# Bidirectional scan of a Mamba-2 layer: where the decay exponents are built, and by which engine

## The reference

```python
a_cs = jnp.cumsum(dt * a_head, axis=2)
seg = a_cs[:, :, :, None] - a_cs[:, :, None, :]
decay = jnp.exp(jnp.where(lower, seg, -jnp.inf))
y_diag = einsum(cb[..., None] * decay, x * dt)
chunk_states = einsum(bmat, decay_end, x * dt)
y_off = einsum(cmat, s_in, jnp.exp(a_cs))
y = y_f + flip(y_b) + xs * p['d'][:, None]
y = y * silu(z)
```

## Time and profile before

| | us |
|---|---|
| median of 3 runs | 1374.57 (1373.78 to 1378.78) |
| the profiled execution, its own time | 1375.81 |
| its span in the profile | 1374.0 |
| PE busy in the span | 1204.2 (88%) |
| DVE busy | 805.6 (59%) |
| ACT busy | 649.9 (47%) |
| POOL busy | 523.4 (38%) |

### The profile page before, as it was taken

How to read it: one execution, slowest core, us unless ns; L and a number is a source line. 1 busy time by engine, 2 the same in 40 slices (tenths; PEclk the granted TensorE clock), 3 DMA queues, 4 the chain that set the end, 5 groups by cost and what they waited for, 6 DMA issues and landing times.

```text
span 1374.0 us, 17386 instructions
## 1 busy us (share of the span) xinstructions
PE 1204.2 (88%) x6304; PEld 951.4 (69%) x6304; DVE 805.6 (59%) x1047; ACT 649.9 (47%) x1131; POOL 523.4 (38%) x233
## 2 busy tenths in 40 slices
PE   4799878877899999999789999677778889999998
PEld 1675453447567877778689999555557866777778
DVE  2546894473247887874467710687864024688782
ACT  2524113363425666765465533656644132466661
POOL 0513220022005545455135554577644500545650
PEclk9799798988999999999899999877789999899999
DMA  8644149940226888884113333544410302688961
GB/s 352 234 153 153 62 175 357 422 167 1 107 96 229 298 285 316 275 279 179 70 64 123 123 123 123 130 127 130 145 54 1 153 16 104 213 284 304 321 241 46
DMA packets 80031, 241.68 MB, mean 176 GB/s; under 512 B 6624, under 2 KB 38880, under 8 KB 67168
## 3 DMA queue, kind: packets, MB, share of 16 engines
q1 hardware_dynamic: 76336, 235.43, 48.3%
q10 hardware_dynamic: 3632, 5.42, 1.2%
HBM read 236.36 MB, written 4.46 MB: 175 GB/s over the span
## 4 chain that ended last, share of the span: by engine, by line
PE 56%; issue 12%; DVE 11%; POOL 7%; ACT 7%; DMA 6%; SPq 1%; ACTq 0%; DVEq 0%; POOLq 0%
PE bank L1887 10%; PE bank L1889 9%; PE bank L1888 9%; POOL wlo L667 4%; PE bank L2396 4%; PE bank L1911 3%; PE bank L2145 3%; DMA raw<-experts 3%; PE bank L2269 2%; POOL wlo L650 2%; DVE wlo L1630 2%; PE bank L2154 2%; PE bank L1955 2%; DVE ct L1767 1%; ACT whi L769 1%
## 5 line engine op out<-in xcount | busy, mean ns | idle before, releaser
L650 POOL TENSOR_TENSOR wlo<-raw,whi 128x2048 fp32r<-128x2048 f32 x39 | 178.7, 4586 | 360.9 <-ACT whi L769 360.9
L1630 DVE TENSOR_TENSOR wlo<-raw,whi 128x1024 fp32r<-128x1024 f32 x144 | 251.7, 1772 | 37.0 <-ACT whi L1004 35.5
L1004 ACT CAST whi<-raw 128x1024 fp32r<-128x1024 f32 x216 | 225.4, 1052 | 97.1 <-PE bank L1889 48.5
L667 POOL TENSOR_TENSOR wlo<-raw,whi 128x1024 fp32r<-128x1024 f32 x72 | 203.2, 2823 | 170.3 <-ACT whi L1004 170.3
L1887 PE MATMUL bank<-hhi,whi 128*128 128x384 f32 (+1 forms) x504 | 175.4, 348 | 16.6 <-DVE hlo L1297 7.2
L1888 PE MATMUL bank<-hlo,whi 128*128 128x384 f32 (+1 forms) x504 | 172.8, 343 | 0.0
L1889 PE MATMUL bank<-hhi,wlo 128*128 128x384 f32 (+1 forms) x504 | 172.7, 343 | 0.0
L1887 PE MATMUL bank<-whi,blk_hi 128*128 128x512 f32 x288 | 116.7, 405 | 2.6 <-issue 1.4
L1888 PE MATMUL bank<-wlo,blk_hi 128*128 128x512 f32 x288 | 114.3, 397 | 0.0
L1889 PE MATMUL bank<-whi,blk_lo 128*128 128x512 f32 x288 | 114.0, 396 | 0.0
L1887 PEld LDWEIGHTS bank<-hhi,whi 128*128 128x128 f32 (+1 forms) x504 | 95.6, 190 | 26.7 <-issue 10.8
(11 more groups left out here) (340 smaller groups left out, 2348.4 us busy)
## 6 DMA issues: line engine op xcount, KB each, us to landing
raw<-experts SPq DMA_DIRECT2D x216, 512.0 KB, 4.8
raw<-stream SPq DMA_DIRECT2D x61, 1024.0 KB, 4.9
modw<-core_mods SPq DMA_DIRECT2D x32, 1024.0 KB, 8.4
rowb<-acs_rows SPq DMA_DIRECT2D x48, 256.0 KB, 4.9
shared<-shared SPq DMA_DIRECT2D x6, 1024.0 KB, 7.9
s<-s0T SPq DMA_DIRECT2D x8, 256.0 KB, 4.3
new_s<-pf SPq DMA_DIRECT2D x16, 128.0 KB, 3.5
x<-xT ACTq DMA_DIRECT2D x1, 1536.0 KB, 13.7
```

Source lines behind the costliest of these rows:

```text
L650: pool.tensor_tensor(wlo[:, q % SPL, :], raw[:, pos % RAW, :], whi[:, q % SPL, :].bitcast(F32), ALU.subtract).then_inc(lo_done, 1)
L667: pool.tensor_tensor(unit(wlo, j), unit(raw, j), unit(whi, j).bitcast(F32), ALU.subtract).then_inc(ls.e_lo[j % SLOTS], 1)
L1004: act.copy(unit(whi, j), unit(raw, j)).then_inc(ls.e_hi, 1)
L1630: dve.tensor_tensor(unit(wlo, j), unit(raw, j), unit(whi, j).bitcast(F32), ALU.subtract).then_inc(ls.e_lo[j % SLOTS], 1)
```

## The change

- The exponents are no longer clamped on DVE. The cumulative sums and log(dt) minus them are written, each as a rounded part and a rest, to DRAM (`lines_out`, `nb_out`; one new PE job `nbT`), and SP brings per group 10 rows for each tile into `lines_f` (`fetch_lines`, six small transfers; one constant table of 74x1280 once). ACT rounds them into `lines` (`lines_cast`).
- PE `differences(n)` makes, for each direction, the exponent of four heads in PSUM by a product over ten rows, and adds a table `never` (0 or -1e30) by a product with the identity, so that the triangle is in the exponent. For t above 0 a product over two rows broadcasts the cumulative sum into another bank. Banks 4 to 7 hold these; the scan's jobs have four banks instead of six.
- ACT makes one exponential of 128x512 per direction out of PSUM into `seg`, and one into `ce` for t above 0. `seg` has two buffers instead of three.
- The C-B product is copied once, without triangle (`cb`).
- The skip term leaves PE: DVE `skipped` adds D times x to the result (two scalar_tensor_tensor of 128x128), and `gated` multiplies by z one tile later.
- Of `weighted_x`, the two products of tile 0 move from POOL to ACT (`scaled_x`, eight of 128x64); POOL does its other two at t = 2. POOL's quarter steps of weights go two at a time at t = 0.
- `turned(0)` and `differences(0)` stand before the last pair of z (`zw7`).

```diff
-    add(turned(0) + states(0))
+    add(numbered("xs", 8) + ["nbT"] + numbered("xs", XCH)[8:])
+    add(numbered("z", XCH)[:14] + turned(0) + numbered("z", XCH)[14:] + states(0))
...
+        b = turn % (CORE_BANKS if n in core else SCAN_BANKS if n in scan else JOB_BANKS)
...
-SOW_AT = {9: "sow3", 16: "sow4", 23: "sow5"}
+SOW_AT = {6: "sow3", 12: "sow4", 18: "sow5"}
...
+    def fetch_lines(hg):
+        for t in range(TILES):
+            ts = slice(t * P, (t + 1) * P)
+            at = 32 * t
+            sp.dma_start(lines_f[at:at + 2, 0:1024].rearrange("p (h l) -> p h l", h=8),
+                         rows_dram[8 * hg:8 * hg + 8, :, ts].rearrange("h a l -> a h l")).then_inc(lines_in, 16)
+            sp.dma_start(lines_f[at + 2:at + LINE_K, 1024:].rearrange("p (d l) -> p d l", d=2),
+                         cols_dram[8 * hg:8 * hg + 8, :, ts].rearrange("(d h) a l -> (h a) d l", d=2)).then_inc(
+                lines_in, 16)
...
-    sp.wait_ge(acs_out, 16)
-    taken(sp, JOB["z15"])
-    fetch_rows(0)
-    fetch_rows(1)
+    sp.wait_ge(lines_stored, 32)
+    sp.dma_start(lines_f[0:LINE_ROWS, :], inp["lines"]).then_inc(lines_k_in, 16)
+    sp.wait_ge(lines_k_in, 16)
+    fetch_lines(0)
+    sp.wait_ge(conv_out, 24)
     fetch_state(0)
+    sp.wait_ge(lines_set, 1)
+    fetch_lines(1)
     for n in range(TILES * 2 * SSD_G):
         hg, t = divmod(n, TILES)
-        if n >= 2:
-            finished(sp, JOB[f"y{(n - 2) // TILES}_{(n - 2) % TILES}"])
-        if n + 2 < TILES * 2 * SSD_G:
-            fetch_rows(n + 2)
+        finished(sp, JOB[f"y{hg}_{t}"])
+        if t == 1 and hg + 2 < 2 * SSD_G:
+            sp.wait_ge(lines_set, hg + 2)
+            fetch_lines(hg + 2)
...
+        if t == 2 and hg + 1 < 2 * SSD_G:
+            weighted_x(hg + 1)
+        if t == 0 and hg < 6:
+            for _ in range(2):
+                low_step(SPLIT_NO["sow0"] + nlow_steps // LOW_STEPS, nlow_steps % LOW_STEPS)
+                nlow_steps += 1
...
+    def scaled_x(hg):
+        if hg:
+            finished(act, JOB[f"st{hg - 1}_1"])
+        for dr in range(2):
+            for i in range(4):
+                h = dr * 32 + 4 * hg + i
+                w = slice(i * 64, (i + 1) * 64)
+                ins = act.activation(xw[:, dr, w], xtok[:, hg % 2, 0, w], ACT.Identity, bias=0.0,
+                                     scale=wdt[:, 0, h:h + 1])
+            ins.then_inc(xw_scaled, 1)
+    def lines_cast(hg):
+        act.wait_ge(lines_in, 16 * 2 * TILES * (hg + 1))
+        act.copy(lines[0:LINE_ROWS, hg % 2, :], lines_f[0:LINE_ROWS, :]).then_inc(lines_set, 1)
+    act.wait_ge(lines_stored, 32)
     turned_out(0)
+    split_to("sow0")
+    lines_cast(0)
+    z_out(7)
+    act.wait_ge(wdt_ready, 1)
+    taken(act, JOB["xt0_1"])
+    scaled_x(0)
+    split_to("sow2")
+    for n in range(TILES * 2 * SSD_G):
+        hg, t = divmod(n, TILES)
+        if n >= SEGS:
+            finished(act, JOB[f"y{(n - SEGS) // TILES}_{(n - SEGS) % TILES}"])
+        for dr in range(2):
+            act.wait_ge(seg_made, 2 * n + dr + 1)
+            act.activation(seg[:, n % SEGS, dr, :], bank[SEG_BANK + dr][:, :], ACT.Exp).then_inc(seg_exp, 1)
             if t:
+                act.wait_ge(row_made, (hg * 2 + t - 1) * 2 + dr + 1)
+                act.activation(ce[:, n % SEGS, dr, :], bank[CE_BANK + dr][:, :], ACT.Exp).then_inc(row_exp, 1)
+        if t == 0:
+            if hg:
+                act.wait_ge(pf_out, 32 * hg)
+            out_of(f"st{hg}_0", (pf[:, :], bk(JOB[f"st{hg}_0"])[:, 0:512]))
+        if t == 1 and hg + 1 < 2 * SSD_G:
+            turned_out(hg + 1)
+            taken(act, JOB[f"xt{hg + 1}_0"])
+            scaled_x(hg + 1)
+            lines_cast(hg + 1)
...
+    def skipped(hg, t):
         n = JOB[f"y{hg}_{t}"]
         ts = slice(t * P, (t + 1) * P)
         finished(dve, n)
+        for c in range(2):
+            ins = dve.scalar_tensor_tensor(xf[:, 2 * hg + c, ts], xf[:, 2 * hg + c, ts],
+                                           v("ssd_d", 2 * hg + c, 1), bk(n)[:, c * P:(c + 1) * P],
+                                           ALU.mult, ALU.add)
+        took(ins, n)
+    def gated(hg, t):
+        ts = slice(t * P, (t + 1) * P)
         both = slice(2 * hg, 2 * hg + 2)
+        taken(dve, JOB[f"y{hg}_{t}"])
+        dve.tensor_tensor(xf[:, both, ts], xf[:, both, ts], z[:, both, ts], ALU.mult).then_inc(y_ready, 1)
...
+    turned_cb(0)
     for n in range(TILES * 2 * SSD_G):
         hg, t = divmod(n, TILES)
         for dr in range(2):
             dve.wait_ge(seg_exp, 2 * n + dr + 1)
             s4 = seg[:, n % SEGS, dr, :].rearrange("p (h l) -> p h l", h=4)
-            dve.tensor_tensor(s4, s4, cbm[:, dr, t, :].unsqueeze(1).to_broadcast([P, 4, P]),
+            dve.tensor_tensor(s4, s4, cb[:, t, :].unsqueeze(1).to_broadcast([P, 4, P]),
                               ALU.mult).then_inc(seg_masked, 1)
+            if dr == 0 and n >= 2:
+                gated((n - 2) // TILES, (n - 2) % TILES)
         if n % 6 == 5 and hg + 1 < 2 * SSD_G:
-            masked_cb(n // 6 + 1)
+            turned_cb(n // 6 + 1)
+        if t == 0:
+            decayed(hg)
         if n:
-            gated((n - 1) // TILES, (n - 1) % TILES)
-        if n + 2 < TILES * 2 * SSD_G:
-            clamped(n + 2)
+            skipped((n - 1) // TILES, (n - 1) % TILES)
         if t == 0:
             next_state(hg)
+    gated(2 * SSD_G - 1, TILES - 2)
+    skipped(2 * SSD_G - 1, TILES - 1)
...
+    def differences(n):
+        hg, t = divmod(n, TILES)
+        if t == 0:
+            pe.wait_ge(lines_set, hg + 1)
+        at = 32 * t
+        for dr in range(2):
+            dst = bank[SEG_BANK + dr]
+            if n:
+                pe.wait_ge(seg_exp, 2 * (n - 1) + dr + 1)
+            pe.matmul(dst[:, :], lines[at:at + LINE_K, hg % 2, 1024 + dr * P:1024 + (dr + 1) * P],
+                      lines[at:at + LINE_K, hg % 2, dr * 512:(dr + 1) * 512],
+                      start=True, stop=False)
+            pe.matmul(dst[:, :].rearrange("p (h l) -> p h l", h=4), ident_r[:, :],
+                      never[:, dr, :].unsqueeze(1).to_broadcast([P, 4, P]), start=False,
+                      stop=True).then_inc(seg_made, 1)
+            if t:
+                before = (hg * 2 + t - 1) * 2 + dr
+                if before >= 2:
+                    pe.wait_ge(row_exp, before - 1)
+                else:
+                    pe.wait_ge(bank_taken[CE_BANK + dr], USES_BEFORE_SCAN[CE_BANK + dr])
+                pe.matmul(bank[CE_BANK + dr][:, :], lines[at:at + 2, hg % 2, 1024 + dr * P:1024 + (dr + 1) * P],
+                          lines[at:at + 2, hg % 2, dr * 512:(dr + 1) * 512], start=True, stop=True).then_inc(row_made, 1)
     turned(0)
+    pe.wait_ge(masks_ready, 2)
+    differences(0)
+    pair("zw7", [JOB["z14"], JOB["z15"]], hhi, hlo)
     states(0)
     for hg in range(2 * SSD_G):
+        differences(TILES * hg + 1)
         outputs(hg, 0)
         if hg + 1 < 2 * SSD_G:
             turned(hg + 1)
+        differences(TILES * hg + 2)
         outputs(hg, 1)
+        if hg + 1 < 2 * SSD_G:
+            differences(TILES * hg + 3)
```

292 lines of the change are left out of this document (138 added, 154 removed).

## The result

The changed kernel took **1402.1 us** in the median of 4 runs (1394.4 to 1405.4), beside 1374.3 of the kernel before on the same chip: a ratio of 1.019, 95% interval 1.016 to 1.022. It is slower, by 27.8 us where 8.8 were predicted, and lies above the range. The profiled execution took 1405.4 with a span of 1403.5 us, 29.5 longer than the span before.

A forecast was written before the change was run, and what follows sets the result against it. The prediction took the z projections as bound by PE and the scan by waits. Start 10.9, groups 1.4, end -4.6, `skipped` 0.7 and `nbT` 0.4 made +8.8 us, forecast 1383; range 1367 to 1397.

The forecast's parts named there:

- The start: From z13's end to the first state copy: PE's last z pair queues behind table, lines and cast, costing 10.9 us.
- I put the table at 858.7: At the start: the 379 KB constant table, issued behind the load of `sow2`, lands at 858.7, bounds 857.1 and 861.
- One group now: Each scan group: a 16.4 us chain through ACT, PE and POOL plus 2.1 for the clock, 18.5 against 18.3; seven groups, +1.4.
- `differences` for t = 1, six of 0.235, 1.4: In each group's chain: six 512-column PE matmuls at 0.235 us, scaled from the 0.18 pitch of 384 columns.
- I cost its edits at nothing within a group: DVE in a group: it loses six clamps, is near no limit, and its edits hide behind ACT and POOL, 0 us.
- the thing that I had named as what would prove me wrong: Among the signs of being wrong: the chain goes through DVE in the scan; no size given.
- I give it no case of its own: DVE and POOL excluding each other for whole instructions: POOL's products for t = 2 take 3.9 us, program 8.8 longer, 1392.
- The clock term: In each group: PE idleness drops the clock in 7 of 10 groups, 6 us at half speed, 2.1 us a group.
- The end: Last group: no `turned`, `scaled_x` or cast, so 9.8 us in place of 14.4, -4.6; two `skipped` before gating add 0.7.
- A: Rival, chance 0.20: differences break PE's idle stretch, the clock stays up, a group takes 16.4 us, total 1366 to 1367.
- B: Rival, chance 0.15: DVE waits for the state's transfer, issued behind six line transfers; 2 us a group, 14 more, 1397.
- C: Rival, chance 0.15: the start costs little because lines or the `sow2` load come early; 8 us less, 1375, no change.

The follow-up runs named there:

- table_128: The changed kernel with the constant table sent as 128 rows instead of 74: 1393.0 us, ratio 1.013.
- never_only: The changed kernel without the ten-row product of every difference: group 19.01 us; the whole, 1433.8 us, is not comparable because outputs were altered.
- skip_out: The changed kernel with the skip term left out and the product with z reading PSUM again: group 18.33 us, whole 1391.5 us, ratio 1.012.
- combo0: The changed kernel with a 128-row table, table and first lines before `zw6`, gate behind masks and `skipped`, tile-0 x products on POOL: 1361.4 us, ratio 0.991.
- combo: combo0 with the first lines' cast earlier, the next lines' cast behind tile 2's exponentials, casts of `sow1` and `sow2` moved into groups: 1351.9 us, ratio 0.983.

## Why the prediction was wrong

The direction and the places were right: a dearer start, a slightly longer group, a shorter end. The failed step is the size of two terms, the start and the group, and one mechanism in the second: that DVE's edits cost nothing within a group.

**"The start".** 15.9 us in place of 10.9. Of the chain that I wrote down every member is there, and most are near their figures: cast 1.27 for 1.24, `scaled_x` 2.0 for 2.2. The table is not: "I put the table at 858.7 (bounds 857.1 ... and 861)". It landed 11.56 us after its issue, at 866.6, 2.3 us of it because this run stood later. I scaled from rows of other shapes by bytes and did not ask about this one's, of which the packets went two at a time. table_128 gives 5.9, as predicted, and 5.1 us back, and 30.1 - 19.3 = 10.8 is my sum. In part that is luck, since two errors cancel in it: in table_128 six issues and the last landing took 3.0 us for my 4.8, and PE from the first difference to z15 13.1 for my 11.9.

**"One group now".** 19.86 in place of 18.5, 10.1 us over seven groups in place of 1.4.

- "`differences` for t = 1, six of 0.235, 1.4": it is 2.37, five at 0.42 or 0.43. The pitch of 384 columns in the earlier trace rows was of matmuls whose weights load while the one before runs; scaling it by columns carried that over to a row of products of which five in six wait 0.18 for their own weights. This is +1.0 where all six are on the chain, as at 974.09; in the group before that, DVE's route is on it instead. never_only shows 0.4 to 0.9 for the ten-row products' share.
- "I cost its edits at nothing within a group" is the mechanism that was wrong. DVE is indeed less busy than before, but the share was not the question. The gate was put between two masks, and it had become an operation that waits for POOL. The chain went through mask, gate and mask on DVE, the thing that I had named as what would prove me wrong. skip_out shows 1.5 us a group, 1.1 at the least.
- "I give it no case of its own: ... the longest product, 1.72, is shorter than 1.25 + 0.70". The row was read wrongly. An engine that finds the other's instruction begun waits only for what is left of it, so a product may take anything from 1.25 to 1.95 by that rule, and 1.72 is 1.25 and 0.47 of a mask. The masks of the kernel before, 1112 ns in the mean where 0.70 is one alone, showed it plainly: it was DVE's side that had to be looked at.
- The clock term, 2.1 us a group, was near, in part by luck: outputs t = 2 took 2.4 to 3.7 for 1.98 and `states` up to 3.1 for 1.93, 1.8 us a group in the mean of seven. Its reason, an idle stretch of over 2 us ahead of the outputs of t = 2, came in four groups; in others stops of 0.97 were enough, and a fall came in all seven, not in 7 of 10.
- The errors do not simply add, since 1.0 and 1.5 are more than the 1.4 missed. From 953.65 to 974.09, a group of 20.4 us, DVE's route took 5.9 us up to `turned` where I had 2.6 for differences and outputs, and 5.0 from the cast to the outputs of t = 2 where I had 4.0; ACT's and the clock's terms were a little smaller than mine.

**"The end".** -1.3 us in place of -3.9. One us of that is a slip in the sum: its terms, 1.4, 1.7, 5.6 and 2.1, make 10.8 and not 9.8, handoffs apart, so -4.6 should have been -3.6, and the forecast 1384.4. For the rest, in the last group the chain is DVE's alone for 7.8 us, to 1041.12 (the last mask's rest left out):

```profile
1033.33 0.69 DVE seg L1908
1034.02 1.42 DVE xf L1868
1035.44 1.69 DVE seg L1908
...
1037.64 1.46 DVE seg L1908
1039.10 1.41 DVE xf L1868
```

It is the same failed step. In combo0, with the gates behind, POOL's two products are the last instead, and the end takes 13.0.

**The rivals.** A did not come in this kernel, but its numbers are those of combo0 and combo, by other edits: groups of 16.0 to 16.2 at a clock of 0.94 to 0.97, close to A's 16.4. B did not: DVE waited for the state's transfer 1.5 us in all. C did not; with the table early the start is 24.9, still 5.6 more than before where C had 2.9. The four cases had no place for a transfer of twice the length and a DVE route as long as POOL's, and neither did the range.
